# State-space output projection in two passes by token halves, with three transformed inputs made in its second pass

## The chip, the cores and the metric

The kernel runs on one core of a Trainium2 chip. The core has a matrix engine (TensorE, PE in the profile; its weight loads are listed apart as PEld), VectorE (DVE), ScalarE (ACT), GpSimd (POOL) and SyncE (SP), whose queue issues all the DMA transfers. The metric is the time of one execution on the device in microseconds (us).

## The reference

Two transformer-like blocks follow each other on 1024 tokens of width 1024, in 32-bit floats. The part that matters here is in the second block: a state-space branch and an attention branch are projected, gated and merged.

```python
proj = jnp.einsum("bsd,de->bse", h, w_in)
z_ssm, xbc, dt_raw, q, k, v, z_att, f_logit, g_logit = jnp.split(proj, offsets, axis=-1)
y_ssm = _ssd_branch(z_ssm, xbc, dt_raw, conv_w, conv_b, dt_bias, a_log, d_skip, ssm_norm_w)
y_att = _fox_branch(q, k, v, z_att, f_logit, b_f)
g_ssm, g_att = jnp.split(jax.nn.sigmoid(g_logit + b_gate), N_BRANCHES, axis=-1)
merged = g_ssm * jnp.einsum("bse,ed->bsd", y_ssm, w_proj_ssm) + g_att * jnp.einsum("bse,ed->bsd", y_att, w_proj_att)
x = x + gate[:, None, :] * jnp.einsum("bsd,de->bse", merged, w_out)
```

`_ssd_branch` ends with `_rmsnorm(y * silu(z), ssm_norm_w)`. The `gate` above is the last third of `silu(c) @ w_ada + b_ada` (the modulation).

## The kernel before

Activations lie with the 128 channels of a block on the partitions and the 1024 tokens along the free dimension. A product of 32-bit accuracy is made from three fast ones: each operand is split into a high part (rounded, on ScalarE) and a low part (the rest, on VectorE or GpSimd), and `mm3` (three calls of `mm`, L344) adds high*high, high*low and low*high.

**Weights** come as one long list of blocks (`weight_plan`), each [128, 8, 128] (512 KB) for an input width of 1024. `w_load(i)` brings block i into one of two raw buffers once the low part of block i-2 is made. `w_hi(i)` (L328) waits for the load and for the last matmul of block i-2, as there are two buffers for the high parts as well. `w_lo(i)` (L335, here on GpSimd) waits for `w_hi(i)`. `lin(i, hf, ...)` gives the 24 matmuls of block i for one half of the tokens (512).

**The order** within each engine is written out by hand; engines meet at semaphores. A function like `w_hi(PSM[n] + 2)` in a list makes its engine wait there, and whatever stands behind it waits as well. PSUM has eight banks, handed out in turn (`next_bank`); a bank is free once the engine that reads it has read it.

**The state-space output projection** (`stage_ssm_out`) follows the scan (`stage_ssd`). TensorE multiplies the gate block `GS` for both halves, each followed by one matmul that sums squares for the norm (`total`), and then the eight blocks of the projection, `PSM[0]` to `PSM[7]`, each for both halves. ScalarE first makes the high parts of the 16 scaled inputs (L2536), then for each half the sigmoid of the gate (L2543) and the norm factor `rstd` (Ln at L409, Exp at L411), with a split of weights between the halves, and then one `w_hi` per block. VectorE makes the 16 low parts (L2558), scales each product out of PSUM (L2570) and adds up the modulation in eight steps (`ada_step`, L428 and L431), whose sums TensorE makes with eight small matmuls after block 5 (`ada_sums`, read at L446). Results go to DRAM (`md`), one store per half block.

**The gathering stage** (`stage_seven`) computes nine pairs of blocks of `w_in` (attention gate z, and gate logits). Each pair is a product of [2 halves of width] x [2 blocks] by [2 halves of width] x [2 halves of tokens], made with seven products instead of eight: P1, P2, P7, P6, P4, P3, P5. A product is 12 matmuls of 512 tokens. P1, P2 and P3 use the input as it is; P7, P6, P4 and P5 use transformed inputs, sums and differences of its quadrants (`quadrant` L2700, `combine` L2706 on VectorE, `x_hi` L2711 on ScalarE, `x_lo` L2717 on VectorE), which are made once and serve all nine pairs. The weights are summed likewise (`weight_add`, VectorE) and split (`weight_hi` L2685 on ScalarE, `weight_lo` L2691 on GpSimd) into four slots. P7's transformed input is made in the projection stage after block 5; P6, P4 and P5 are made in the gathering stage, as their buffers lie where the projection's split inputs `YS` lie. To bridge that, the order of products starts with P1, P2, P7 of pair 0 and then of pair 1. The load of pair 1 (`pair_load(1)`, L2646) waits for the end of the projection.

Of the kernel before, what the change touches and what calls it, by code (L numbers as in the profile page):

```python
# [43 lines left out]
def weight_plan():  # L44
# [65 lines left out]
    add("gs", W, None, 1024, (G_LOG, G_LOG + 128))  # L110
    full("ps", "w_proj_ssm_2", None, 1024, 0, 8)
# [79 lines left out]
def program(nc, io, table):  # L191
    xT, pT, wflat, wada, vecs, rows, cst, abias, tabs, out = io
    stack = ExitStack()
    with stack:
# [2316 lines left out]
        YS = Y([P, 8, T], F32R), Y([P, 8, T], F32R)  # L2511

        def stage_ssm_out():
            GS, PSM = BLK["gs"][0], BLK["ps"]
            T_ = tmps([((n, hf), (f"md{(2 * n + hf) % 4}", n, hf)) for n in range(8) for hf in range(2)])
# [16 lines left out]

            def scalar():
                for hf in range(2):
                    for k in range(8):
                        ac.activation(YS[0][:, k, half(hf)], XS[:, k, half(hf)], ACT.Identity, scale=v("ssn", k)).then_inc(*on.up(ac, "uh", "S", k, hf))  # L2536
                for hf in range(2):
                    if hf:
                        w_hi(GS + 2)
                    to, before = T_[0, hf]  # L2540
                    on.wait_ge(ac, "mm", GS, hf)
                    on.wait_ge(ac, *before)
                    ac.activation(to, ps[:, bank[GS, hf], :], ACT.Sigmoid, bias=bgn[:, 0:1]).then_inc(*on.up(ac, "gate s", hf))  # L2543
                    rstd("S", hf, bank["S", hf], RA, T)
                for n in range(8):
                    w_hi(PSM[n] + 2)
                    if n == 6:
                        for j in range(2):
                            x_hi("P7", j)
                        for x in range(2):  # L2550
                            weight_hi(x)
                on.ends(ac, "end ssm", "ac")

            def vector():
                for hf in range(2):
                    for k in range(8):
                        on.wait_ge(dv, "uh", "S", k, hf)
                        dv.scalar_tensor_tensor(YS[1][:, k, half(hf)], XS[:, k, half(hf)], v("ssn", k), YS[0][:, k, half(hf)], ALU.mult, ALU.subtract) \  # L2558
                            .then_inc(*on.up(dv, "ul", "S", k, hf))
                for n in range(8):  # L2560
                    for hf in range(2):
# [919 lines left out]
```

## Time and profile before

| What | Value |
|---|---|
| Median of 3 runs | 2794.96 us (2793.74 to 2798.78) |
| The profiled execution, its own time | 2794.93 us |
| Its span, first to last instruction | 2793.6 us |
| TensorE (PE) busy | 2697.8 us, 97% |
| VectorE (DVE) busy | 1683.9 us, 60% |
| ScalarE (ACT) busy | 1388.7 us, 50% |
| GpSimd (POOL) busy | 910.7 us, 33% |
| TensorE's mean granted clock | 0.990 |

The granted clock is TensorE's clock as a share of 2.4 GHz; it has two levels, 1.2 and 2.4 GHz. Matmuls are pipelined and their ends are modelled, so busy times of PE overlap; its gaps are what to look at. Times in the rows are counted from the first instruction.

### The profile page before, as it was taken

Reading aid. Unit: us, or ns where it says so; the run is one execution under the profiler, and the core shown is the slowest. Engines: PE = TensorE matmul, PEld = TensorE weight load, DVE = VectorE, ACT = ScalarE, POOL = GpSimd, SP = SyncE. Lnnn points to the kernel's source line nnn. Section 1 sums busy time; section 2 is a strip of 40 time slices with the busy share of each in tenths; the row PEclk is TensorE's granted clock in tenths of the full one; section 3 lists DMA queues with packets and bytes.
Section 4 is the critical chain, followed back from the end, with each engine's and each line's share of the span. In section 5 each row is a group of like instructions: output and inputs, shape, how many; then the busy total and the mean of one; then the engine's idle time right before and its main releaser. Section 6 shows DMA issues by size and latency. Waiting matters only on the chain.

```text
span 2793.6 us, 36562 instructions
## 1 busy us (share of the span) xinstructions
PE 2697.8 (97%) x13692; PEld 2250.3 (81%) x13692; DVE 1683.9 (60%) x2861; ACT 1388.7 (50%) x2550; POOL 910.7 (33%) x745
## 2 busy tenths in 40 slices
PE   8999989999999999999998999998999999999997
PEld 7878878777788888888886778777788888888886
DVE  6767775643288888887557875556552444443344
ACT  5768864435367767775346335542442343334222
POOL 0434441223366655563122221123541111111431
PEclk9999999999999999999999999999999999999999
DMA  3101132221100000003211310033342110010242
GB/s 136 42 31 42 42 125 70 85 83 39 38 13 10 11 11 10 11 31 113 74 48 35 114 38 23 23 128 106 113 147 93 47 33 29 31 31 31 83 151 76
DMA packets 62367, 167.68 MB, mean 60 GB/s; under 512 B 7024, under 2 KB 15856, under 8 KB 61040
## 3 DMA queue, kind: packets, MB, share of 16 engines
q1 hardware_dynamic: 62192, 165.34, 17.3%
q8 instruction: 111, 1.82, 0.3%
q14 instruction: 64, 0.52, 0.1%
HBM read 139.10 MB, written 26.21 MB: 59 GB/s over the span
## 4 chain that ended last, share of the span: by engine, by line
PE 88%; DVE 5%; ACT 3%; POOL 2%; issue 1%; DMA 0%; POOLq 0%; ACTq 0%; DVEq 0%
PE ps L344 82%; PE ps L462 4%; PE ps L3012 1%; PE ps L788 1%; ACT t L328 1%; POOL t L1328 1%; POOL t L1332 1%; POOL t L1780 0%; DVE t L3370 0%; DMA t<-in_wflat 0%; DVE t L2338 0%; DVE t L919 0%; DVE t L888 0%; POOL t L1330 0%; DVE t L1907 0%
## 5 line engine op out<-in xcount | busy, mean ns | idle before, releaser
L344 PE MATMUL ps<-t,t 128*128 128x512 f32 (+8 forms) x11804 | 2539.4, 374 | 71.3 <-POOL t L2691 10.3
L344 PEld LDWEIGHTS ps<-t,t 128*128 128x128 f32 (+4 forms) x11804 | 2049.5, 185 | 491.4 <-issue 67.4
L335 POOL TENSOR_TENSOR t<-t,t 128x1024 fp32r<-128x1024 f32 (+2 forms) x151 | 323.8, 2145 | 1102.8 <-ACT t L328 746.8
L328 ACT ACTIVATE t<-t 128x1024 fp32r<-128x1024 f32 (+2 forms) x187 | 167.9, 898 | 413.0 <-PE ps L344 412.5
L1720 DVE TENSOR_TENSOR t<-ps,t 128x512 fp32r<-128x512 f32 x256 | 164.6, 684 | 33.2 <-ACT t L1628 32.0
L1780 POOL TENSOR_SCALAR t<-t,t 128x1024 f32<-128x1024 f32 x128 | 144.3, 1127 | 118.7 <-DVE t L1726 113.7
L462 PE MATMUL ps<-t,t 128*128 128x128 f32 x1176 | 157.5, 274 | 11.9 <-POOL t L1780 9.6
L462 PEld LDWEIGHTS ps<-t,t 128*128 128x128 f32 x1176 | 132.4, 140 | 31.1 <-issue 15.2
L1733 DVE TENSOR_REDUCE t<-ps 128x1 f32<-128x1024 f32 x128 | 154.2, 1205 | 0.6 <-PE ps L344 0.6
L1636 ACT ACTIVATE t<-ps,t 128x1024 f32<-128x1024 f32 x128 | 143.0, 1117 | 3.5 <-DVE t L1733 3.3
L1628 ACT ACTIVATE t<-ps 128x512 fp32r<-128x512 f32 x256 | 139.1, 591 | 9.8 <-PE ps L462 5.8
L2691 POOL TENSOR_TENSOR t<-t,t 128x512 fp32r<-128x512 f32 x63 | 90.1, 1437 | 88.8 <-ACT t L2685 88.8
L966 POOL TENSOR_SCALAR t<-t,t 128x384 f32<-128x384 f32 (+1 forms) x128 | 69.6, 564 | 126.5 <-DVE t L913 126.5
L1267 POOL TENSOR_TENSOR t<-t,t 128x512 f32<-128x512 f32 x31 | 49.7, 1604 | 143.2 <-DVE t L1176 143.2
L3135 DVE TENSOR_TENSOR t<-ps,t 128x128 fp32r<-128x128 f32 (+3 forms) x64 | 48.4, 757 | 73.9 <-ACT t L3048 73.8
L2685 ACT ACTIVATE t<-t 128x512 fp32r<-128x512 f32 x63 | 39.0, 629 | 79.6 <-PE ps L344 47.4
L827 ACT ACTIVATE t<-t,t 128x384 f32<-128x384 f32 (+1 forms) x128 | 73.9, 581 | 3.3 <-DVE t L897 2.8
L1328 POOL TENSOR_TENSOR t<-t,t 32x512 f32<-32x512 f32 x34 | 43.7, 1287 | 75.7 <-DVE t L1323 75.5
L3048 ACT ACTIVATE t<-ps 128x128 fp32r<-128x128 f32 (+3 forms) x64 | 41.8, 653 | 51.6 <-PE ps L3012 51.6
L2474 ACT ACTIVATE t<-ps,t 128x128 f32<-128x128 f32 x128 | 34.9, 384 | 59.0 <-PE ps L344 52.9
L888 DVE CUSTOM_DVE_ANT_0 t<-ps,t 128x384 f32<-128x384 f32 (+1 forms) x128 | 61.2, 519 | 4.1 <-PE ps L344 3.4
L335 DVE TENSOR_TENSOR t<-t,t 128x1024 fp32r<-128x1024 f32 (+1 forms) x36 | 31.6, 879 | 46.8 <-ACT t L328 46.7
(245 smaller groups left out, 2538.8 us busy)
## 6 DMA issues: line engine op xcount, KB each, us to landing
t<-in_wflat SPq DMA_DIRECT2D x138, 512.0 KB, 3.6
t<-in_wada SPq DMA_DIRECT2D x48, 256.0 KB, 4.8
t<-in_wflat SPq DMA_DIRECT2D x9, 1024.0 KB, 5.9
t<-in_xT SPq DMA_DIRECT2D x16, 512.0 KB, 7.3
md<-t SPq DMA_DIRECT2D x30, 256.0 KB, 2.7
t<-md SPq DMA_DIRECT2D x30, 256.0 KB, 3.9
t<-in_wflat SPq DMA_DIRECT2D x32, 128.0 KB, 2.0
hd<-t SPq DMA_DIRECT2D x8, 512.0 KB, 3.1
```

The costliest lines, as they stand in the source:

```text
L328: ac.activation(parts(i)[0][:, 0:n], raw[i % 2][:, 0:n], ACT.Copy).then_inc(*on.up(ac, "whi", i))
L335: e.tensor_tensor(lo[:, 0:n], raw[i % 2][:, 0:n], hi[:, 0:n], ALU.subtract) \
L344: return pe.matmul(o, l, r, start=start, stop=stop)
L462: t = pe.transpose(o[:, c * P:(c + 1) * P], src[:, c * P:(c + 1) * P], ident)
L827: ac.activation(S[:, r, 0:nk], S[:, r, 0:nk], ACT.Exp, bias=M[:, 8 + r:9 + r], accum_out=M[:, 16 + r:17 + r]) \
L1328: po.tensor_tensor(ta[64:96], ta[64:96], tb[64:96], ALU.add).then_inc(*on.up(po, "roped", *key, 0))
L1628: ac.activation(to, src, ACT.Copy).then_inc(*on.up(ac, "b pT_hi", i - 3, c))
L1636: ac.activation(Pm[u][:, :], o, ACT.Exp, bias=bm[:, c0:c0 + 1], accum_out=bm[:, c0 + 1:c0 + 2]).then_inc(*on.up(ac, "b exp", i - 1))
L1720: dv.tensor_tensor(to, src, turned(i - 3, c, 0)[0], ALU.subtract).then_inc(*on.up(dv, "b pT_lo", i - 3, c))
L1733: dv.tensor_reduce(bm[:, c0:c0 + 1], o, AX, ALU.max, negate=True).then_inc(*on.up(dv, "b max", i))
L1780: po.tensor_scalar(Pm[u][:, :], Pm[u][:, :], bm[:, c0 + 2:c0 + 3], 1.0, ALU.mult, ALU.mult).then_inc(*on.up(po, "b probs", i - 1))
L2691: po.tensor_tensor(lo[:, :, :], weight(p, W_QUAD[q]), hi[:, :, :], ALU.subtract).then_inc(*on.up(po, "seven_po", p, q))
```

## The change

The projection runs in two passes, one for each half of the tokens. In a pass come the gate block, the sum of squares and the eight projection blocks, each for its half alone (`half_block`, 24 matmuls). The weight list therefore has the gate block and the eight projection blocks twice. The split inputs `YS` become two pairs of buffers, one for each half, so that the first half's buffers are free after the first pass; the transformed inputs P6 and P4 lie there, and are made in the second pass after P7. Only P5 is made in the gathering stage. The order of products becomes the plain one, pair after pair. Both `pair_load(0)` and `pair_load(1)` are issued in the second pass. The slots for split weights move, so that only the first is free before the projection ends: only P1's weights are split ahead.

```diff
-    add("gs", W, None, 1024, (G_LOG, G_LOG + 128))
-    full("ps", "w_proj_ssm_2", None, 1024, 0, 8)
+    for hf in range(2):
+        add("gs", W, None, 1024, (G_LOG, G_LOG + 128))
+        full("ps", "w_proj_ssm_2", None, 1024, 0, 8)
...
-        YS = Y([P, 8, T], F32R), Y([P, 8, T], F32R)
+        YS = [(Y([P, 8, H], F32R), Y([P, 8, H], F32R)) for _ in range(2)]
...
+            def half_block(i, hf, hi, lo, need, frees):
+                nk, m, wh, wl = block(i)
+                b = bank[i] = next_bank(*every)
+                on.wait_ge(pe, "whi", i)
+                on.wait_ge(pe, low(i), i)
+                wait_bank(b)
+                for k in range(8):
+                    for event in need(k, hf):
+                        on.wait_ge(pe, *event)
+                    t = mm3(ps[:, b, :], wh[:, k, :], wl[:, k, :], hi(k), lo(k), k == 0, k == 7)
+                t.then_inc(*on.up(pe, "mm", i, 1))
+                freed[b] = frees
...
             def tensor():
                 for hf in range(2):
-                    bank[GS, hf] = lin(GS, hf, next_bank(*every), Uh, Ul, need_c, [("gate s", hf)])
+                    half_block(GS[hf], hf, lambda k: Uh[:, k, half(hf)], lambda k: Ul[:, k, half(hf)], need_c, [("gate s", hf)])
                     bank["S", hf] = next_bank(*every)
                     total("S", hf, bank["S", hf], RA, ("acc", "S", 7, hf))
-                for n in range(8):
-                    for hf in range(2):
-                        bank[PSM[n], hf] = lin(PSM[n], hf, next_bank(*every), *YS, need_y, [("ssm", n, hf)])
-                    if n == 5:
-                        ada_sums(next_bank(*every))
+                    for n in range(8):
+                        half_block(PSM[n + 8 * hf], hf, lambda k: YS[hf][0][:, k, :], lambda k: YS[hf][1][:, k, :], need_y, [("ssm", n, hf)])
+                        if hf and n == 0:
+                            ada_sums(next_bank(*every))
+                    on.ends(pe, "ssm half", hf)
...
             def scalar():
 ...
                 for hf in range(2):
-                    if hf:
-                        w_hi(GS + 2)
                     to, before = T_[0, hf]
-                    on.wait_ge(ac, "mm", GS, hf)
+                    on.wait_ge(ac, "mm", GS[hf], 1)
                     on.wait_ge(ac, *before)
-                    ac.activation(to, ps[:, bank[GS, hf], :], ACT.Sigmoid, bias=bgn[:, 0:1]).then_inc(*on.up(ac, "gate s", hf))
+                    ac.activation(to, ps[:, bank[GS[hf]], :], ACT.Sigmoid, bias=bgn[:, 0:1]).then_inc(*on.up(ac, "gate s", hf))
                     rstd("S", hf, bank["S", hf], RA, T)
-                for n in range(8):
-                    w_hi(PSM[n] + 2)
-                    if n == 6:
-                        for j in range(2):
-                            x_hi("P7", j)
-                        for x in range(2):
-                            weight_hi(x)
+                    w_hi(GS[hf] + 2)
+                    for n in range(8):
+                        w_hi(PSM[n + 8 * hf] + 2)
+                        if hf and n in (2, 4, 6):
+                            for j in range(2):
+                                x_hi({2: "P7", 4: "P6", 6: "P4"}[n], j)
+                weight_hi(0)
...
             def vector():
...
+                for n, hf in users:
...
+                    dv.tensor_tensor(to, ps[:, bank[PSM[n + 8 * hf]], :], by, ALU.mult).then_inc(*on.up(dv, "ssm", n, hf))
+                    if hf == 0:
+                        ada_step(n)
+                    elif n == 1:
                         ada_out()
                         for j in range(2):
                             quadrant((1, 1), j, "P7", fh)
                             quadrant((0, 1), j, "P7", fl)
                             combine("P7", j, fh["P7"], fl["P7"], ALU.subtract)
+                    elif n == 2:
+                        for j in range(2):
+                            quadrant((0, 0), j, "P6", fh)
+                            combine("P6", j, fl["P7"], fh["P6"], ALU.add)
                         weight_add(0, "P7")
+                    elif n == 3:
                         for j in range(2):
                             x_lo("P7", j)
+                    elif n == 4:
+                        for j in range(2):
+                            quadrant((1, 0), j, "P4", fl)
+                            combine("P4", j, fl["P4"], fl["P6"], ALU.subtract)
+                    elif n in (5, 6):
+                        for j in range(2):
+                            x_lo({5: "P6", 6: "P4"}[n], j)
...
             def gpsimd():
                 for hf in range(2):
-                    if hf:
-                        w_lo(po, GS + 2)
+                    w_lo(po, GS[hf] + 2)
...
+                    for n in range(8):
+                        if hf and n == 7:
+                            weight_lo(0)
+                        w_lo(po, PSM[n + 8 * hf] + 2)
...
             def sync():
+                w_load(GS[0] + 4)
+                on.wait_ge(sp, "ul", "S", 7, 1)
+                for k in range(3):
+                    ada_load(k)
+                for n, hf in users:
+                    if (n, hf) == (0, 1):
+                        w_load(GS[1] + 4)
+                    w_load(PSM[n + 8 * hf] + 4)
+                    on.wait_ge(sp, "ssm", n, hf)
+                    sp.dma_start(md[n, :, half(hf)], T_[n, hf][0]).then_inc(*on.landed(sp, f"md{n % 4}", n, hf))
+                    if hf == 0 and n < 5:
+                        ada_load(n + 3)
+                    if hf and n in (1, 2):
+                        pair_load(n - 1)
...
-        ORDER = [(p, q) for q in ("P1", "P2", "P7") for p in (0,)] + [(1, "P1"), (1, "P2"), (1, "P7")]
-        ORDER += [(p, q) for q in PRODUCTS[3:] for p in range(2)] + [(p, q) for p in range(2, len(SEVEN)) for q in PRODUCTS]
+        ORDER = [(p, q) for p in range(len(SEVEN)) for q in PRODUCTS]
...
             def scalar():
-                for x in range(2, 4):
+                for x in range(1, 4):
                     weight_hi(x)
...
             def vector():
                 for j in range(2):
+                    quadrant((1, 1), j, "P5", fh)
+                    if j == 0:
+                        weight_add(0, "P6")
+                    dv.tensor_tensor(two(fl["P5"], j), two(xl["P6"], j), two(xh["P6"], j), ALU.add) \
                         .then_inc(*on.up(dv, "seven_dv/again", j))
                     on.wait_ge(dv, "seven_dv/again", j)
+                    combine("P5", j, fh["P5"], fl["P5"], ALU.subtract)
                 for x, (p, q) in enumerate(ORDER):
                     if x + 5 < len(ORDER):
                         weight_add(*ORDER[x + 5])
+                    if x == 2:
+                        for j in range(2):
+                            x_lo("P5", j)
                     add(p, q)
```

## Rows read from the trace of the kernel before

**Rows 1.** The page's chain that ended last, by engine, shares of the span.

```profile
PE 88%; DVE 5%; ACT 3%; POOL 2%; issue 1%; DMA 0%; POOLq 0%; ACTq 0%; DVEq 0%
```

**Rows 2.** Timeline of PE, 1812 to 2200: start, length, what, count, [idle before, releaser].

```profile
1823.79 109.76 PE L344 MATMUL ps<-t,t 128*128 128x512 f32 x476 [2.93 <-DVE t L2394]
1934.50 3.02 PE L344 MATMUL ps<-t,t 128*128 128x512 f32 x12 [0.94 <-POOL t L2691]
1942.38 11.35 PE L344 MATMUL ps<-t,t 128*128 128x512 f32 x36 [4.87 <-POOL t L2691]
1957.71 10.06 PE L344 MATMUL ps<-t,t 128*128 128x512 f32 x36 [3.98 <-POOL t L2691]
...
1968.32 180.67 PE L344 MATMUL ps<-t,t 128*128 128x512 f32 x798 [0.54 <-POOL t L2691]
```

**Rows 3.** Timeline of all engines, where VectorE reads modulation sums and the last product.

```profile
1906.23 0.17 DVE L446 TENSOR_TENSOR t<-ps,t 128x8 f32<-128x8 f32 x1 [0.99 <-PE ps L344]
...
1928.15 0.69 DVE L2570 TENSOR_TENSOR t<-ps,t 128x512 f32<-128x512 f32 x1 [2.17 <-PE ps L344]
```

**Rows 4.** Timeline of all engines at the projection stage's start.

```profile
1828.13 9.94 ACT L2536 ACTIVATE t<-t,t 128x512 fp32r<-128x512 f32 x16 [0.81 <-DVE t L2413]
...
1832.67 5.68 PEld L344 LDWEIGHTS ps<-t,t 128*128 128x128 f32 x25 [0.24 <-issue]
1838.08 1.28 ACT L2543 ACT_TABLE_LOAD   x1
...
1839.02 94.11 PEld L344 LDWEIGHTS ps<-t,t 128*128 128x128 f32 x423 [0.24 <-issue]
1839.38 0.69 ACT L2543 ACTIVATE t<-ps,t 128x512 f32<-128x512 f32 x1
...
1843.92 1.05 ACT L328 ACTIVATE t<-t 128x1024 fp32r<-128x1024 f32 x1
...
1845.43 2.40 POOL L335 TENSOR_TENSOR t<-t,t 128x1024 fp32r<-128x1024 f32 x1
```

**Rows 5.** The same timeline, load of pair 1 and its first user.

```profile
1933.59 0.48 SPq L2646 DMA_DIRECT2D t<-in_wflat  x1
...
1940.36 0.63 ACT L2685 ACTIVATE t<-t 128x512 fp32r<-128x512 f32 x1 [10.56 <-DMA t<-in_wflat]
```

**Rows 6.** Windows: length, busy us (count) of PE, PEld, DVE, ACT, POOL, granted clock, DMA share, GB/s.

```profile
1824.00:1826.00 2.00, 2.00 (x5) 1.58 (x6) 2.00 (x5) 0.00 (x0) 0.00 (x0) 0.50 0.00 0
1860.00:1870.00 10.00, 10.00 (x46) 8.29 (x45) 6.86 (x8) 1.06 (x1) 2.40 (x1) 1.00 0.79 254
```

**Rows 7.** Timeline of ACT in the scan stage, a table load and its first use.

```profile
1800.29 1.28 ACT L2474 ACT_TABLE_LOAD   x1
1802.17 2.18 ACT L2474 ACTIVATE t<-ps,t 128x128 f32<-128x128 f32 x8 [0.59 <-PE ps L344]
```

**Rows 8.** Timeline of all engines, end of one projection block and the next split.

```profile
1882.79 0.69 DVE L2570 TENSOR_TENSOR t<-ps,t 128x512 f32<-128x512 f32 x1 [3.43 <-PE ps L344]
1882.85 1.07 ACT L328 ACTIVATE t<-t 128x1024 fp32r<-128x1024 f32 x1 [9.82 <-PE ps L344]
...
1883.99 2.41 POOL L335 TENSOR_TENSOR t<-t,t 128x1024 fp32r<-128x1024 f32 x1 [8.47 <-ACT t L328]
```

**Rows 9.** The same timeline, VectorE and GpSimd together, then each alone (1936.70 and 1941.06).

```profile
1929.36 2.88 POOL L335 TENSOR_TENSOR t<-t,t 128x1024 fp32r<-128x1024 f32 x1 [4.00 <-ACT t L328]
1930.02 3.30 DVE L2847 TENSOR_TENSOR t<-t,t 128x1024 f32<-128x1024 f32 x1
1932.20 2.25 POOL L2691 TENSOR_TENSOR t<-t,t 128x512 fp32r<-128x512 f32 x1
...
1936.70 1.22 DVE L2847 TENSOR_TENSOR t<-t,t 128x1024 f32<-128x1024 f32 x1
...
1941.06 1.27 POOL L2691 TENSOR_TENSOR t<-t,t 128x512 fp32r<-128x512 f32 x1 [6.62 <-ACT t L2685]
```

**Rows 10.** Groups by line and form, 1826 to 1990: count | busy, mean ns | idle before.

```profile
L2700 DVE TENSOR_TENSOR t<-t,t 128x1024 f32<-128x1024 f32 x10 | 15.4, 1538 | 0.1
```

More of the change, by code:

```diff
@@ L2510, in program @@
         Y = region(YO)
-        YS = Y([P, 8, T], F32R), Y([P, 8, T], F32R)
+        YS = [(Y([P, 8, H], F32R), Y([P, 8, H], F32R)) for _ in range(2)]
         def stage_ssm_out():
-            GS, PSM = BLK["gs"][0], BLK["ps"]
-            T_ = tmps([((n, hf), (f"md{(2 * n + hf) % 4}", n, hf)) for n in range(8) for hf in range(2)])
+            GS, PSM = BLK["gs"], BLK["ps"]
+            users = [(n, hf) for hf in range(2) for n in range(8)]
+            T_ = tmps([((n, hf), (f"md{n % 4}", n, hf)) for n, hf in users])
             need_y = lambda k, hf: [("uh", "S", k, hf), ("ul", "S", k, hf)]
@@ L2626, in program @@
         S7 = region(OO + 16384)
-        slots = [(S7([P, 4, P], F32R), S7([P, 4, P], F32R)) for _ in range(2)]
-        pair_raw = [S7([P, 2 * T])]
+        pair_raw = [S7([P, 2 * T]) for _ in range(2)]
         S7 = region(YO + 49152)
-        pair_raw.append(S7([P, 2 * T]))
-        slots += [(S7([P, 4, P], F32R), S7([P, 4, P], F32R)) for _ in range(2)]
         scaled = [S7([P, H]) for _ in range(2)]
+        spare = [(S7([P, 4, P], F32R), S7([P, 4, P], F32R)) for _ in range(4)]
+        slots = [spare[3]] + spare[0:3]
         tiles = [t[:, :] for t in tmp] + [RA[:, half(hf)] for hf in range(2)]
-        ORDER = [(p, q) for q in ("P1", "P2", "P7") for p in (0,)] + [(1, "P1"), (1, "P2"), (1, "P7")]
-        ORDER += [(p, q) for q in PRODUCTS[3:] for p in range(2)] + [(p, q) for p in range(2, len(SEVEN)) for q in PRODUCTS]
+        ORDER = [(p, q) for p in range(len(SEVEN)) for q in PRODUCTS]
         def pair_load(p):
-            if p == 0:
-                on.wait_ge(sp, "ul", "S", 7, 1)
-            elif p == 1:
-                on.wait_ge(sp, "end ssm", "pe")
+            if p < 2:
+                on.wait_ge(sp, "sums/ada", 2)
             else:
@@ L2676, in weight_hi @@
                 on.wait_ge(ac, "mm/seven", *ORDER[x - 4])
-            elif x < 2:
-                on.wait_ge(ac, "sums/ada", 2)
-            else:
+            elif x:
                 on.wait_ge(ac, "end ssm", "pe")
@@ L2696, in quadrant @@
         def quadrant(x, j, q, to):
+            if q in ("P6", "P4"):
+                on.wait_ge(dv, "ssm half", 0)
             kh, hf = x
@@ L2738, in before_tile @@
                     return [stored[y][mine - 1]]
-                return [(f"md{x}", 6 if x < 2 else 7, x % 2) for x in range(4)] + [("ssm", 7, 1)]
+                return [(f"md{x}", 4 + x, 1) for x in range(4)] + [("ssm", 7, 1)]
             def tensor():
@@ L2778, in scalar @@
             def scalar():
-                for x in range(2, 4):
+                for x in range(1, 4):
                     weight_hi(x)
-                for j in range(2):
-                    x_hi("P6", j)
-                    ac.activation(two(kept, j), two(fl["P6"], j), ACT.Copy).then_inc(*on.up(ac, "seven_ac/keep", j))
                 for x, (p, q) in enumerate(ORDER):
@@ L2789, in scalar @@
                     if x == 1:
-                        for j in range(2):
-                            x_hi("P4", j)
-                    if x == 4:
                         for j in range(2):
@@ L2875, in gpsimd @@
             def gpsimd():
-                for x in range(2, len(ORDER)):
+                for x in range(1, len(ORDER)):
                     weight_lo(x)
@@ L2880, in sync @@
             def sync():
-                pair_load(1)
                 for x in range(4):
-                    on.wait_ge(sp, f"md{x}", 6 if x < 2 else 7, x % 2)
+                    on.wait_ge(sp, f"md{x}", 4 + x, 1)
                 for g in range(2):
```

66 lines of the change are left out of this document (14 added, 52 removed).

## The prediction

> **What bounds the kernel now.** I read the chain that ended last first: TensorE is 88% of it, 82% by the one line that issues the three-term matmuls [rows 1]. So the edit pays or costs by what it does to gaps and clock of TensorE, since it removes no matmul. Next TensorE's timeline around the change [rows 2]. From 1823.79 it runs without a gap through the whole projection and into the gathering stage. Then come gaps of 0.94, 4.87, 3.98 and 0.54 us, and after 1968.32 none for 180 us: 798 matmuls in 180.67 us, 0.2264 us each. One half block (24 matmuls) is thus 5.43 us and one product of the gathering stage (12) 2.72 us.
>
> The projection's last product is taken by VectorE at 1928.15 [rows 3], so TensorE left it at 1928.1; what runs on to 1933.5 are P1 and P2 of pair 0, whose weights were split early. From 1928.1 to 1968.3 are 40.2 us for 2 + 12/12 + 36/12 + 36/12 = 9 products, 24.5 us of work. **15.7 us are lost at the start of the gathering stage**: this is what the edit can win back. 10.3 are gaps. The rest is clock: 36 matmuls took 11.35 and 10.06 us after the long gaps [rows 2] for 8.15 at full rate. The 4.87 us gap is the load of pair 1, issued at 1933.59 and used by ScalarE at 1940.36 [rows 5]; the 3.98 us gap stands before the first P6.
>
> **Part A: one half block instead of two before block 1.** In the stage's first 15 us TensorE has the gate block's first half (to 1832.25, a total to 1832.67), its second half and total (to 1839.02) [rows 4]. These, and the first projection block's two halves, now cover ScalarE, which makes 16 scaled inputs (1828.13 to 1838.07), then table load, sigmoid, table load, Ln, table load, Exp, and only then splits the next weights (1843.92) [rows 4]. In the new order TensorE has only one gate half and one projection half ahead of that split. It is done at 1832.67 + 5.43, with a little for the inputs' arrival 1838.4. The new order puts the split behind the whole gate chain, where it already stands for this first one, and GpSimd now takes the low part before the gate's product: high part 1843.92 to 1844.97, low part 2.40 us long [rows 4], ready at 1847.5. **Gap 9.1 us.** Nothing covers it: the block after is behind it in order. Then the clock: it was at its lower level (0.50, 1.2 GHz) when TensorE resumed at 1823.79 [rows 6], after a gap of 2.93 us [rows 2]; the gate half took 8.46 us for 5.43, a loss of 3.0, and after 4.87 and 3.98 us the losses were 3.2 and 1.9 [rows 2]. I take 2.7. Sum of A: 11.8 us.
>
> **Double weight work in pass 1.** Nine more blocks of 512 KB: nine splits of 1.06 us on ScalarE and 2.40 on GpSimd, and nine loads on SP. Before, both came once per 10.9 us; now each 5.43. After the matmul two blocks earlier ends, the high part takes 0.06 + 1.07, the low one follows at 1.20 and ends at 3.61 us [rows 8], against 5.43 needed. Both are hidden, with 1.8 us to spare. A load leaves 3.6 us after one block's end and is used two blocks later, 7.3 us on. Per block now go 512 KB of weights, 512 of modulation and 256 of output; the window from 1860 moved 254 GB/s at a DMA share of 0.79 [rows 6], hence an estimated 321 GB/s when full, 4.1 us for 1.31 MB. So the double loads are costed at nothing; what they cost if that cover goes is rival 3.
>
> **Part B: the second gate.** The gate half ends, and sigmoid to end of low part is 1839.38 to 1844.97 plus 0.1 plus 2.40 = 8.1 us [rows 4]. Its first table load comes before its wait, as at 1800.29, where the load stands ahead of 0.59 us of waiting for TensorE [rows 7]. TensorE has a total (0.42), one half (5.43) and the modulation sums (1.7: read at 1906.23, after 0.99 us of waiting and 0.69 for the product before them [rows 3]) to set against it: 7.55. Gap 0.6 us, and no clock is lost (0.94 and 0.54 cost next to none [rows 2]).
>
> **Part C: VectorE's new work in pass 2.** It makes P7 (six operations), P6 and P4 (four each) and their low parts (six): 20 of 128x1024 at 1.22 us each when alone [rows 9], 24.4 us, beside GpSimd's 2.40 us split now in every block. The rows show how the two meet. GpSimd's split from 1929.36 took 2.88 us, the VectorE operation issued at 1930.02 took 3.30 for 1.22 and ended 1.08 us after the split's end, and GpSimd's 1.27 us operation [rows 9] of 1932.20 took 2.25. They take turns whole. So while both have work VectorE gets one or two operations per block.
> The Trainium skill, SBUF — State Buffer, "SBUF: two separate sides", says that the pair of ports which the two share is an exclusive lock, and that the loser blocks for the full instruction when VectorE's operation has two SBUF inputs. By this rule the sum comes to the 2810.7 below, and without it to the 2799.4 of rival 1; the rows of contention here agree with it.
> By the mean of the grouped row (1.54 us, [rows 10]) P7 would take 9.2 us and VectorE nearly keep up. By turns it takes 12.1. Block 8 ends at 1847.5 + 2.7 + 9 x 5.43 + 0.4 = 1899.5 and block 9, which starts after the gap of part B at 1901.8, at 1907.3. VectorE takes that product and the sums, starts P7 at 1908.2, gives way at 1909.5 and 1914.2 for 2.4 us each, and ends it at 1920.2. ScalarE has P7's high part queued ahead of the split for block 13, and that split wanted to start at 1918.2. Behind P7's second high part it starts at 1921.3, GpSimd waits out one more VectorE operation, and the low part is there at 1925.9. TensorE is done at 1923.6. **Gap 2.3 us**, clock loss between none (0.94 us gap) and 1.9 (3.98 us gap): 0.8. Later splits wait one VectorE operation at most, 3.61 + 1.22 = 4.8 us after the block's end of 5.43, and are hidden. The projection then ends at 1925.9 + 3 x 5.43 = 1942.2, 1943.0 with the clock: 14.9 us later than 1928.1 (A, B and C give 15.5; the rest is rounding of the blocks before).
>
> **Part D: the start of the gathering stage.** Here the 15.7 us go, and other waits come. By the same turns (one or two operations of 1.22 us, then one split of 2.40) VectorE still owes P4, two pairs of low parts and three products when TensorE ends; P4 is done 2.6 us after that end. ScalarE's P4 high part, the split of the next stage's weights (1.06) and P1's high part (0.6), each queued behind the other, end 5.2 us after it. P1's low part on GpSimd, 1.27 and up to 1.22 behind VectorE, makes 7.0: before, P1 and P2 ran at once. Next, P2's weights stand behind a 2.40 us split: 1.0 more beyond a P1 at low clock. P6's weight sum adds 0.2. VectorE's backlog pushes P5's inputs, and behind them the sum for P3's weights, to some 28 us after the end: gap 3.4. P5's low part 0.7. Clock after the 7.0: 2.7; after the 3.4: 1.0. Sum 16.0, against 15.7 now: +0.3. From pair 1 on, whose load is now early (issued in pass 2), all is as before.
>
> **Sum.** A 11.8 + B 0.6 + C 3.1 + D 0.3 = 15.8 us on the profiled execution's 2794.93 (span 2793.6), which is the median of the three runs to 0.03 us: 2810.7.
>
> **The rivals.** Rival 1, VectorE keeps up, by the grouped mean of 1.54 us. Then there is no gap in C, and D is P1's split chain behind block weights (1.06 + 0.1 + 0.6 + 1.27, 3.1 us), 2.7 of clock and some 2 for P2 and P6: 7.8, 7.9 less than now. Result 12.4 - 7.9 = +4.5, 2799.4. For it: that mean is what these operations took here. Against it: GpSimd worked less often when they did. It decides once VectorE ends its list with TensorE: some 10 us less than by turns.
> Rival 2, not slower: the gathering stage's start loses nothing, all seven transformed inputs and weights waiting when TensorE comes. The 15.7 us come back whole, and A and B take 12.4: -3.3, 2791.6, within 0.2%. The start may lose up to 15.7 - 12.4 + 5.6 = 8.9 us before the result is slower by 0.2%. Against it: P2's high part still waits for the stage's end by its own line, and VectorE's list is 25 us long without any turn taken.
> Rival 3, pass 1 starves: weights come late while the modulation loads share the queue. It bites from 7.3 us between issue and landing; each of five blocks then waits about 1 us: 2816, and with VectorE's backlog growing to two operations more, 2819. For it: the share of 0.79 with half the weights. Against: 4.1 us of 5.43.
>
> **Chances.** Forecast 0.61 (own range 2805 to 2817: A's clock by 1, C's 0 to 1.9, D by 4). Rival 1 0.17, rival 2 0.09, rival 3 0.13. Range 2797 to 2820, which leaves out rival 2 and the ends of the rest. A change of 0.2% is 5.6 us, about what a measurement can tell from none. Slower holds the forecast, rival 3 and half of rival 1: 0.83. The same holds the rest of rival 1 and most of rival 2: 0.13. Faster 0.04.
>
> **What would show it.** In the changed kernel's trace: a TensorE gap of about 9 us ended by GpSimd's low part near 1847.5, with low clock after it; one under 1 us near 1902; one of 2 to 3 us near 1924, with ScalarE waiting for VectorE's P7; then about 7 us at the first product of the gathering stage and 3 us at its sixth; no wait for a pair's load. If instead the first gap is under 6 us, ScalarE's order is not what I read. If VectorE's transforms average 1.3 us, rival 1 holds. A load that TensorE waits for in pass 1 is rival 3.

## The result, and the profile after

The changed kernel took 2805.49 us (median of 6 runs, 2803.69 to 2806.65) against 2796.03 us for the kernel before (6 runs, 2793.74 to 2798.78): a ratio of 1.0033, 95% interval 1.002 to 1.0046, 9.5 us more. The forecast was 2811, 15.8 more, with 2797 to 2820 as its range: slower as said, by three fifths of the amount.

TensorE's timeline after the change, to be read against [rows 2] (start, length, what, count, [idle before, releaser]):

```profile
1825.88 14.40 PE L345 MATMUL ps<-t,t 128*128 128x512 f32 x50 [2.92 <-DVE t L2395]
1849.68 76.36 PE L345 MATMUL ps<-t,t 128*128 128x512 f32 x330 [9.40 <-POOL t L336]
1927.30 16.56 PE L345 MATMUL ps<-t,t 128*128 128x512 f32 x72 [1.26 <-ACT t L329]
1948.21 16.70 PE L345 MATMUL ps<-t,t 128*128 128x512 f32 x60 [4.35 <-POOL t L2708]
1967.55 193.08 PE L345 MATMUL ps<-t,t 128*128 128x512 f32 x846 [2.65 <-POOL t L2708]
```

Look for four gaps. Two stand in the projection, where there was none before: TensorE waits 9.40 us for GpSimd's low part of block 1, and 1.26 us at block 13. Two stand at the start of the gathering stage, where there were four before: 4.35 us for P1's low part and 2.65 us for P3's. (Blocks are counted as in the prediction: 0 to 7 are the first pass's eight projection blocks, 8 to 15 the second pass's.) Both kernels do the same products from the gate block's first matmul to the gathering stage's last one, so this stretch can be laid side by side: 1968.32 + 180.67 - 1823.79 = 325.20 us before [rows 2], 1967.55 + 193.08 - 1825.88 = 334.75 us after, 9.55 more. This is the measured difference of the medians. The profiled spans differ by 11.7 us (2793.6 and 2805.3), 2.1 more, since the stretch began at 1825.88 instead of 1823.79: nothing is changed ahead of it, and the start varied between 1822.89 and 1827.70 over the profiles below. So I compare stretches, and medians beside them.

The place of the first gap, all engines, to be read against [rows 4]:

```profile
1830.21 9.93 ACT L2552 ACTIVATE t<-t,t 128x512 fp32r<-128x512 f32 x16 [0.81 <-DVE t L2414]
...
1840.16 1.28 ACT L2557 ACT_TABLE_LOAD   x1
1841.45 0.69 ACT L2557 ACTIVATE t<-ps,t 128x512 f32<-128x512 f32 x1
...
1845.99 1.99 ACT L329 ACTIVATE t<-t 128x1024 fp32r<-128x1024 f32 x2
1847.19 2.34 POOL L336 TENSOR_TENSOR t<-t,t 128x1024 fp32r<-128x1024 f32 x1 [24.53 <-ACT t L329]
```

ScalarE has work without a pause from 1830.21 to 1847.98, and block 1's split stands at the end of its list. TensorE had done block 0 at 1840.28 and waits for the low part at 1849.53. And the second pass, where VectorE and GpSimd meet:

```profile
1910.44 4.55 DVE L2719 TENSOR_TENSOR t<-t,t 128x1024 f32<-128x1024 f32 x2
1910.96 2.95 POOL L336 TENSOR_TENSOR t<-t,t 128x1024 fp32r<-128x1024 f32 x1 [3.44 <-ACT t L329]
...
1916.16 4.55 DVE L2719 TENSOR_TENSOR t<-t,t 128x1024 f32<-128x1024 f32 x2
...
1916.40 3.23 POOL L336 TENSOR_TENSOR t<-t,t 128x1024 fp32r<-128x1024 f32 x1 [2.49 <-ACT t L329]
...
1920.75 1.23 DVE L2725 TENSOR_TENSOR t<-t,t 128x1024 f32<-128x1024 f32 x1
...
1922.01 1.06 ACT L2730 ACTIVATE t<-t 128x1024 fp32r<-128x1024 f32 x1 [4.67 <-DVE t L2725]
...
1922.97 1.04 ACT L329 ACTIVATE t<-t 128x1024 fp32r<-128x1024 f32 x1
...
1946.10 1.65 ACT L2702 ACTIVATE t<-t 128x512 fp32r<-128x512 f32 x3
1946.79 1.36 POOL L2708 TENSOR_TENSOR t<-t,t 128x512 fp32r<-128x512 f32 x1 [3.72 <-ACT t L2702]
```

Two VectorE operations of 1.22 us each take 4.55 where a split by GpSimd falls among them, and GpSimd's split of 2.40 takes 2.95 and 3.23. ScalarE waits 4.67 us for P7 (1922.01) with block 13's split behind it (1922.97). The same meeting is seen in VectorE's making of P4, twice in this stretch:

```profile
1935.62 2.82 DVE L2719 TENSOR_TENSOR t<-t,t 128x1024 f32<-128x1024 f32 x1
...
1940.86 3.30 DVE L2725 TENSOR_TENSOR t<-t,t 128x1024 f32<-128x1024 f32 x1
```

Grouped over 1826 to 1990, the quadrants took 2.17 us each where [rows 10] had 1.54:

```profile
L2719 DVE TENSOR_TENSOR t<-t,t 128x1024 f32<-128x1024 f32 x10 | 21.7, 2168 | 0.1
```

### The profile page after: what moved, and what is told of

It reads as the page before. It is cut to its first block, busy times and chain, and to the rows that moved or that the text cites. A ratio compares the mean times of both kernels' runs of the same rounds, so it can differ in the third digit from the quotient of the medians.

```text
span 2805.3 us, 36614 instructions
## 1 busy us (share of the span) xinstructions
PE 2704.1 (96%) x13692; PEld 2253.8 (80%) x13692; DVE 1693.5 (60%) x2861; ACT 1396.1 (50%) x2557; POOL 933.9 (33%) x754
## 3 DMA queue, kind: packets, MB, share of 16 engines
q8 instruction: 111, 1.82, 0.3%
## 4 chain that ended last, share of the span: by engine, by line
PE 84%; DVE 6%; POOL 4%; ACT 3%; issue 2%; DMA 1%; SPq 0%; POOLq 0%; DVEq 0%; ACTq 0%
PE ps L345 77%; PE ps L463 4%; PE ps L3018 1%; POOL t L336 1%; PE ps L789 1%; DMA t<-md 1%; DVE t L2719 1%; ACT t L329 1%; DMA t<-gd 1%; POOL t L1329 1%; POOL t L1333 1%; POOL t L1781 0%; DVE t L3376 0%; ACT t L2552 0%; DVE t L2725 0%
## 5 line engine op out<-in xcount | busy, mean ns | idle before, releaser
L336 POOL TENSOR_TENSOR t<-t,t 128x1024 fp32r<-128x1024 f32 (+2 forms) x160 | 350.0, 2188 | 1121.9 <-ACT t L329 764.9
L329 ACT ACTIVATE t<-t 128x1024 fp32r<-128x1024 f32 (+2 forms) x196 | 177.1, 905 | 401.3 <-PE ps L345 400.8
```

The costliest lines, as they stand in the source:

```text
L329: ac.activation(parts(i)[0][:, 0:n], raw[i % 2][:, 0:n], ACT.Copy).then_inc(*on.up(ac, "whi", i))
L336: e.tensor_tensor(lo[:, 0:n], raw[i % 2][:, 0:n], hi[:, 0:n], ALU.subtract) \
```

## The experiments

All stand beside runs of the kernel before on the same chip, so two kernels are compared by their ratios, or by each one's distance from the kernel before, and not by their bare medians. "Stretch" is the 325.20 us above, of the one profiled run. Edits are shown against the changed kernel.

| Kernel | Median, us | Before beside it | Ratio (95%) | Stretch, against before |
|---|---|---|---|---|
| changed kernel | 2805.49 | 2796.03 | 1.0033 (1.002 to 1.0046) | +9.55 |
| e1_split_first | 2794.97 | 2796.44 | 0.9997 (0.9988 to 1.0006) | -1.10 |
| e2_fill_gap | 2812.16 | 2796.44 | 1.0058 (1.0045 to 1.0072) | +10.60 |
| e2b_fill_same_bank | 2805.91 | 2795.59 | 1.0033 (1.0021 to 1.0045) | +8.96 |
| e3_short_lows | 2799.34 | 2796.44 | 1.0013 (1.0004 to 1.0022) | +3.23 |
| e4_passes_alone | 2809.37 | 2796.44 | 1.005 (1.0038 to 1.0063) | +13.61 |
| e5_start_order | 2809.82 | 2795.59 | 1.0051 (1.0038 to 1.0063) | +12.18 |
| e5b_load_out_of_way | 2803.78 | 2794.63 | 1.0033 (1.0021 to 1.0046) | +7.63 |
| e7_all_orders | 2800.81 | 2795.59 | 1.0016 (1.0008 to 1.0025) | +1.82 |
| e7b_all_orders_2 | 2791.22 | 2794.63 | 0.9987 (0.9978 to 0.9996) | -5.75 |
| e8_p7_high_later | 2804.99 | 2795.59 | 1.0032 (1.002 to 1.0045) | +9.53 |

**Is the first gap ScalarE's order?** The splits of blocks 1 and 2 go ahead of the gate chain, in the second pass that of block 9 does too, and GpSimd's low parts follow in the same order.

```diff
                 for hf in range(2):
                     for k in range(8):
...
+                    w_hi((GS[0], PSM[0])[hf] + 2)
                 for hf in range(2):
+                    if hf:
+                        w_hi(GS[1] + 2)
...
                     rstd("S", hf, bank["S", hf], RA, T)
-                    w_hi(GS[hf] + 2)
```

> The changed kernel with ScalarE's order alone altered: the splits of weight blocks 1 and 2 stand behind the first and the second eight scaled inputs, ahead of the gate chain; in pass 2 block 9's split stands ahead of the gate chain too (GpSimd's low parts follow in the same order). Theory 1 (the 9.4 us gap is ScalarE's order and nothing else): 8 inputs end 5.0 us after 1830.2, high part 1.06, low part 2.4, so block 1 is ready near 1838.8 + 0.1, before TensorE ends block 0 at 1840.3: gap 0, and with no gap no low clock, so 9.4 + 2.6 = 12.0 us less than the changed kernel, some 2.5 us less than the kernel before; the rest (1.3 us at block 13, start of the gathering stage 11.6 us lost) as it was. Rival (the weights' load or SP's queue stands right behind the split): the gap shrinks only to 4 to 6 us, for the load of block 3 is then what is late. Rival 2 (clock falls whatever the gap): only 9.4 us less.

```profile
1826.16 25.18 PE L345 MATMUL ps<-t,t 128*128 128x512 f32 x98 [2.93 <-DVE t L2395]
1852.14 5.72 PE L345 MATMUL ps<-t,t 128*128 128x512 f32 x24 [0.80 <-issue]
1859.09 57.44 PE L345 MATMUL ps<-t,t 128*128 128x512 f32 x258 [1.23 <-issue]
```

```profile
1855.47 1.06 ACT L329 ACTIVATE t<-t 128x1024 fp32r<-128x1024 f32 x1 [6.25 <-DMA t<-in_wflat]
```

In e1's timeline of TensorE the 9.40 us and the low clock after it are gone; 0.80 and 1.23 us have come in their place, of which the second is the load of block 4 (ScalarE waited 6.25 us for it, to 1855.47), issued behind six modulation loads. The stretch is 10.65 us shorter than the changed kernel's: 12.0 were expected, and 2.0 went to the new gaps. The expectation's first rival, a late load right behind the split, was right about the mechanism and not about its size or its block. The order on ScalarE, and on GpSimd behind it, was worth the whole of the change's net loss: with it mended the kernel is as fast as before.

**Is the gap's second cost the clock?** 38 matmuls that nobody reads fill it.

```diff
+                        if hf == 0 and n == 0:
+                            b = next_bank(*every)
+                            wait_bank(b)
+                            for x in range(38):
+                                mm(ps[:, b, :], idr[:, :], YS[0][0][:, 0, :], x == 0, x == 37)
+                            freed[b] = []
```

> The changed kernel with 38 more matmuls (identity by one scaled input, into a bank nobody reads) after block 0 of pass 1, inside the 9.4 us gap; they add nothing to the output. Theory 1 (the gap's second cost is TensorE's clock, low since it stood still): the clock stays at its upper level, blocks 1 to 3 take 5.43 us each, block 1 ends 8.4 us after block 0's end of waiting instead of 10.7, 2.6 us less than the changed kernel. Rival (block 1's 8.1 us come from waiting for its second operand or from load traffic, not the clock): nothing changes, or it is slower by what the fill overlaps the weights' arrival.

This did not answer the question: `next_bank` moved the turn of the banks for every stage that follows, there was a wait of 1.47 us late in the gathering stage that no other profile has, and the kernel came out 15.7 us slower than before. With the bank kept (`b = every[(turn[every] + 1) % 8]`, and no change to `freed`):

> As e2_fill_gap, but the 38 filling matmuls go into the bank that block 1 then takes and overwrites, so that the turn of the banks in all later stages is that of the changed kernel. Theory 1 (clock): the gap is filled, block 1 takes 5.4 to 5.7 us instead of 8.1, and the stretch from the gate block's start to the attention stage is 1.5 to 2.6 us shorter than the changed kernel's 336.75; e2's later losses (a wait of 1.47 us in the gathering stage and 2.5 us after it) are gone, for they came with the shifted banks. Rival (the fill itself costs later, by load on the memory or the clock): the later losses stay.

Windows (length, busy us and count of PE, PEld, DVE, ACT, POOL, granted clock, DMA share, GB/s), first of the changed kernel, then of e2b:

```profile
1850.00:1854.00 4.00, 4.00 (x10) 3.11 (x10) 0.74 (x2) 0.00 (x0) 3.10 (x2) 0.50 0.77 257
```

```profile
1849.00:1853.00 4.00, 4.00 (x19) 3.31 (x18) 1.10 (x2) 0.00 (x0) 2.86 (x2) 1.00 0.89 285
...
1901.00:1904.00 3.00, 3.00 (x10) 2.33 (x9) 0.69 (x1) 0.00 (x0) 2.83 (x2) 0.57 0.61 175
```

At a clock of 0.50 TensorE began 10 matmuls in 4 us, at 1.00 it began 19. So the clock was the gap's second cost, 8.1 us for block 1 against 5.43. But the stretch is only 0.6 us shorter, not 1.5 to 2.6: the clock now fell at 1901, where in the changed kernel it had stayed up (below), and the medians show no gain at all. The wait of e2 is gone, as expected. Of e2's loss behind the gathering stage 1.5 us are gone, and 1.0 is left against the changed kernel (643.7 us from the attention stage's start to the end, for 645.2 in e2 and 642.7 in the changed kernel; the last section shows where clock was lost there).

**Do VectorE and GpSimd take turns?** The low parts of blocks 10 to 15 are made for 16 columns only; the rest of them is left out.

```diff
                 hi, lo = parts(i)
+                if i in BLK["ps"][10:16]:
+                    n = 16
```

> The changed kernel with the low parts of the weights of blocks 10 to 15 (pass 2) made for 16 of 1024 columns alone; the rest of these low parts is left out, so GpSimd's 2.4 us splits vanish from the stretch in which VectorE makes P7, P6 and P4. Theory 1 (VectorE and GpSimd take turns, whole instructions long): P7's six operations take 7.4 us instead of 11.5, the 1.26 us gap at block 13 is gone, VectorE's list ends before TensorE does, and the start of the gathering stage loses 3.1 us of gap and 2.6 of clock, 5.7 instead of 11.6: 7 us less in all. Rival (VectorE's list is long by itself, no turns): P7 stays near 11 us, at most 1 us less in all.

```profile
1908.44 2.48 DVE L2721 TENSOR_TENSOR t<-t,t 128x1024 f32<-128x1024 f32 x2
...
1910.95 1.23 DVE L2727 TENSOR_TENSOR t<-t,t 128x1024 f32<-128x1024 f32 x1
1912.09 2.48 DVE L2721 TENSOR_TENSOR t<-t,t 128x1024 f32<-128x1024 f32 x2
...
1914.61 1.23 DVE L2727 TENSOR_TENSOR t<-t,t 128x1024 f32<-128x1024 f32 x1
...
1943.70 15.50 PE L347 MATMUL ps<-t,t 128*128 128x512 f32 x60 [3.33 <-POOL t L2710]
```

P7 takes 7.4 us, 1908.44 to 1915.84, for 11.5; block 13 waits no more; the gathering stage's first gap is 3.33 us (3.1 expected) for 4.35. The stretch is 6.3 us shorter than the changed kernel's (7 expected). So GpSimd's splits are what makes VectorE's list long, and the two take turns, as the prediction said; what one turn costs VectorE was 2.1 us and not 2.4.

**What do the passes cost alone, and what do the early transforms repay?**

The projection keeps its two passes; the order of products, the buffers, the load of pair 1 and the making of P6 and P4 go back to those of the kernel before.

```diff
-                        if hf and n in (2, 4, 6):
+                        if hf and n == 6:
                             for j in range(2):
-                                x_hi({2: "P7", 4: "P6", 6: "P4"}[n], j)
-                weight_hi(0)
+                                x_hi("P7", j)
+                            for x in range(2):
+                                weight_hi(x)
...
-        ORDER = [(p, q) for p in range(len(SEVEN)) for q in PRODUCTS]
+        ORDER = [(p, q) for q in ("P1", "P2", "P7") for p in (0,)] + [(1, "P1"), (1, "P2"), (1, "P7")]
+        ORDER += [(p, q) for q in PRODUCTS[3:] for p in range(2)] + [(p, q) for p in range(2, len(SEVEN)) for q in PRODUCTS]
```

> The two passes alone: the kernel before, with its order of products, its buffers, and P6, P4 and P5 made in the gathering stage, but the projection in two passes with the weights loaded twice, P7 made after block 9. Theory 1 (the passes cost, the early transforms repay): TensorE's gap of 9.4 us before block 1 and 2.6 us of clock stay, no gap at block 13, and the start of the gathering stage loses what it lost before, 15.7 us: 12 us more than the kernel before, 2.5 us more than the changed kernel. Rival (early transforms do not repay, their gain is lost at VectorE): 9.5 us more than the kernel before or less, that is no slower than the changed kernel.

```profile
1849.41 92.81 PE L345 MATMUL ps<-t,t 128*128 128x512 f32 x402 [9.27 <-POOL t L336]
1942.69 5.74 PE L345 MATMUL ps<-t,t 128*128 128x512 f32 x24 [0.48 <-POOL t L2705]
1950.56 3.01 PE L345 MATMUL ps<-t,t 128*128 128x512 f32 x12 [2.13 <-POOL t L2705]
1957.77 11.35 PE L345 MATMUL ps<-t,t 128*128 128x512 f32 x36 [4.19 <-POOL t L2705]
1973.10 10.06 PE L345 MATMUL ps<-t,t 128*128 128x512 f32 x36 [3.98 <-POOL t L2705]
```

Against the kernel before it takes 13.6 us more in the stretch, 12.9 in the median: 9.27 us before block 1 and its clock, then gaps of 0.48, 2.13, 4.19, 3.98 and 0.55 us at the start of the gathering stage, 11.3 where the kernel before had 10.3. The early transforms, with the order of products and the loads that go with them, repay 4.1 us in the stretch, 3.5 in the medians (12.9 and 9.5). So they bring more than their gap at block 13 costs; the loss is that of the passes.

**Are the waits at the gathering stage's start queue order?** P1's weights go ahead of P4's high part, the next stage's split behind P6's, P3's sum between P5's halves.

```diff
+                        if hf and n == 6:
+                            weight_hi(0)
...
                 for x in range(1, 4):
                     weight_hi(x)
+                w_hi(PSM_LAST + 2)
...
-                    if j == 0:
-                        weight_add(0, "P6")
+                    weight_add(0, ("P6", "P3")[j])
```

> The changed kernel with the orders at the start of the gathering stage alone altered: P1's weights are split ahead of P4's high part (after block 14), the split of the next stage's weight block comes after the splits of P2, P7 and P6, and the sum for P3's weights is made between the two halves of P5. Theory 1 (the 4.35 us at P1 and the 2.65 us at P3 are queue order on ScalarE, GpSimd and VectorE): no wait at P1 and no low clock there, 0.5 us at P2, about 1 at P6, 2.5 to 3.5 at P5, which still comes late; some 5.5 us lost in place of 11.6, so 6 us less than the changed kernel. Rival (VectorE's backlog of 8.6 us past the end of the projection is what counts): the wait moves from P1 to P7 or P6 whole, and less than 2 us are won.

```profile
1943.66 8.45 PE L345 MATMUL ps<-t,t 128*128 128x512 f32 x36 [1.48 <-POOL t L2711]
1955.06 4.60 PE L345 MATMUL ps<-t,t 128*128 128x512 f32 x12 [2.95 <-POOL t L2711]
1965.94 195.71 PE L345 MATMUL ps<-t,t 128*128 128x512 f32 x858 [6.28 <-POOL t L2711]
```

The expectation was wrong: 2.6 us more in the stretch than the changed kernel instead of 6 less. The gap at P1 fell to 1.48, and 6.28 us came at P4. All engines there:

```profile
1958.34 0.33 SPq L318 DMA_DIRECT2D t<-in_wflat  x1
1958.71 0.43 SPq L2635 DMA_DIRECT2D md<-t  x1
...
1963.42 0.60 ACT L2790 ACTIVATE t<-ps 128x512 f32<-128x512 f32 x1 [9.07 <-DMA md<-t]
```

ScalarE's copy of P1's product waits 9.07 us for the last store to `md`. That store was ready since 1950.9 and stood in SP's queue behind a weight load, which waited for the very split that I had moved to later. The P4 and P3 splits stood behind the copy. With the load moved behind it:

```diff
                 for g in range(2):
                     md_load(g)
+                w_load(PSM_LAST + 4)
```

> As e5_start_order, with one difference: the load of weight block FV0, which in SP's queue stood ahead of the last store to md, comes after the two md loads of the gathering stage. Theory 1 (e5's 6.28 us at P4 is ScalarE's copy of P1's product waiting for that store, which SP held behind a load waiting for the split of FK0 that e5 had moved to later): the copy no longer waits for a DMA, the gap at P4 falls below 1.5 us and the low clock behind it goes; some 6 to 8 us less than e5 (2809.8), 2802 to 2804. Rival (P5's transform on VectorE sets the pace whatever else): the wait moves to P3 or P5 and less than 3 us are won.

```profile
1955.37 4.59 PE L345 MATMUL ps<-t,t 128*128 128x512 f32 x12 [2.95 <-POOL t L2712]
1960.88 5.82 PE L345 MATMUL ps<-t,t 128*128 128x512 f32 x24 [0.92 <-POOL t L2712]
1968.26 188.87 PE L345 MATMUL ps<-t,t 128*128 128x512 f32 x834 [1.55 <-POOL t L2712]
```

The gap at P4 is 0.92 us and the low clock behind it is gone, which settles the cause of e5's loss. The stretch is 4.55 us shorter than e5's. Each set against the kernel before beside it, the medians differ by 5.1 us (9.15 and 14.23 more than it), a little under the 6 to 8 expected. Against the changed kernel the orders win 1.9 us in the stretch, not 6, and only 0.3 in the medians: 2.95 us at P6 remain, whose sum stands behind VectorE's backlog, and 1.55 at P5. The gaps at the gathering stage's start add up to 6.87 us for the changed kernel's 7.00; they have moved, and what was won is clock. So e5's rival, the backlog, holds for the larger part, and the queue's order for the rest.

**Is block 13's gap the split queued behind P7?** P7's high part goes one block later.

```diff
-                        if hf and n in (2, 4, 6):
+                        if hf and n in (3, 4, 6):
```

> The changed kernel with P7's high part on ScalarE moved one block later, behind the split of block 13. Theory 1 (the 1.26 us gap at block 13 is that split queued behind P7): the gap is gone, VectorE's list is as long as before, so 1.3 us less at that place and about as much less in all. Rival (GpSimd's low part is late anyway, behind VectorE's turns): a gap of 0.5 us or more stays.

```profile
1849.09 92.65 PE L345 MATMUL ps<-t,t 128*128 128x512 f32 x402 [9.46 <-POOL t L336]
1947.63 16.73 PE L345 MATMUL ps<-t,t 128*128 128x512 f32 x60 [5.89 <-POOL t L2708]
```

The gap is gone, and nothing is won: 402 matmuls in one piece, and then 5.89 us before P1 instead of 4.35. TensorE finished the projection 1.5 us earlier, counted from its start, and met the same VectorE. The stretch is that of the changed kernel to 0.02 us. A wait that is hidden behind a later one has no price.

**All orders together.** e1, e8 and e5 at once, block 3's split between Ln and Exp, and block 4's load ahead of the modulation.

```diff
+                    if hf == 0:
+                        w_hi(PSM[1] + 2)
                     on.wait_ge(ac, "ln", "S", hf)
...
                 w_load(GS[0] + 4)
+                w_load(PSM[0] + 4)
```

> All orders together: as e1_split_first, with block 3's split between Ln and Exp and the load of block 4 ahead of the modulation loads (e1 had gaps of 0.80 and 1.23 us there), as e8_p7_high_later, and as e5_start_order. Theory 1: no gap in the projection, 2.0 us less than e1 there and 1.3 at block 13, and 5 to 6 less at the start of the gathering stage: 8 us less than e1, 2787 to 2789, 8 to 9 less than the kernel before. Rival (the parts are not additive, since a faster TensorE leaves VectorE's list further behind at the end): only e1's result less 3 to 4 us.

It held e5's fault, 6.26 us at P4, and came out 5.2 us above the kernel before instead of 8 to 9 below. Mended like e5b, with the splits of P2 and P7 ahead of P4's high part, two modulation blocks loaded at first instead of three, and the sums for P6 and P3 made in the projection stage (P6's ahead of P4's low parts; P3's came behind them, though the expectation says ahead):

```diff
+                        if hf and n == 7:
+                            weight_hi(1)
+                            weight_hi(2)
...
+                        if n == 6:
+                            weight_add(0, "P6")
...
-                for k in range(3):
+                for k in range(2):
                     ada_load(k)
```

> As e7_all_orders, with that load moved behind the twelfth product, the split of FK0 moved behind the tenth, the splits of P2's and P7's weights ahead of P4's high part, the sums for P6's and P3's weights ahead of VectorE's last low parts, and two modulation blocks loaded at first instead of three. Theory 1: no gap from the projection's start to P4, one at P5, whose transform VectorE ends about 20 us after the projection's end against 16.3 of products before it: 3 to 7 us and up to 3 of clock. That is 2789 to 2792, 4 to 7 less than the kernel before and 9 to 12 less than e7. Rival (VectorE's backlog only moves on): the gap at P5 is over 9 us, and the result within 2 us of the kernel before.

```profile
1822.89 36.12 PE L345 MATMUL ps<-t,t 128*128 128x512 f32 x146 [2.93 <-DVE t L2395]
1859.28 68.32 PE L345 MATMUL ps<-t,t 128*128 128x512 f32 x306 [0.27 <-issue]
1928.23 8.46 PE L345 MATMUL ps<-t,t 128*128 128x512 f32 x36 [0.63 <-POOL t L2733]
1938.38 3.01 PE L345 MATMUL ps<-t,t 128*128 128x512 f32 x12 [1.70 <-POOL t L2733]
1945.44 196.90 PE L345 MATMUL ps<-t,t 128*128 128x512 f32 x858 [4.05 <-POOL t L2733]
```

It takes 0.9987 of the kernel before (0.9978 to 0.9996), 3.4 us less in the median; the 5.75 us less in the stretch are those of a profiled run near the low end of its eleven (2789.23 us, median 2791.22). So the two passes are a little better than the kernel before once the orders fit them. Whether orders of this kind would speed up the kernel before as well was not run. I had expected one gap, at P5; instead 1.70 us stand at P6 and 4.05 at P4, where ScalarE's copy of P1's product waited 5.49 us for the last store to `md`, whose product VectorE scales behind all of P4's low parts.

## Why the prediction was right, and where it was off

The measured 2805.49 lies in the stated range, just inside the forecast's own 2805 to 2817, and about as far from the forecast's 2810.7 as from rival 1's 2799.4. The number alone does not tell the two apart. The trace and e3 do: VectorE's quadrant operations averaged 2.17 us and not 1.54 in the changed kernel, and P7 took 7.4 us for 11.5 once GpSimd's splits were out of the way. Part by part:

- **Part A**, 11.8 us: 9.40 of gap (9.1 said) and 2.7 of clock (2.7 said; block 1 ran from 1849.68 to 1857.8, 8.1 for 5.43). e1 shows the cause, e2b the clock.
- **Double weight work in pass 1**, nothing: right. From block 1 to block 12 TensorE runs without a gap of 0.3 us, in 76.36 us: 13 x 5.43 = 70.6 of blocks, 0.4 of a total, 1.6 of modulation sums, 2.7 of clock and 1.1 of small delays; the DMA share reached 0.97 in a window from 1854, and no block waited. Rival 3 did not come, though in e1 and e7, where TensorE reaches these blocks sooner, 1.23 and 1.02 us of waiting for a load did.
- **Part B**, 0.6 us: from the gate half's end (1895.84) to block 9's start (1903.99) are 8.15 us, the split chain's 8.1, against 7.55 of work; as a gap only 0.19 of it shows, the rest lies between the small matmuls.
- **Part C**, 3.1 us: 1.26, and no clock (72 matmuls in 16.56 us for 16.30). The mechanism was as said, P7 at 1921.98 with block 13's split behind it, and e8 shows it by taking the gap away; the size was off, in part because a turn costs VectorE 2.1 us and not 2.4, so that P7 took 11.5 us and not 12.1. The prediction's own [rows 9] had this: 3.30 us for an operation of 1.22 is 2.08 more, not 2.40.
- **Part D is the term that was most off**: "Sum 16.0, against 15.7 now: +0.3". TensorE left the projection at 1943.86. From there to 1967.55 are 23.7 us for five products, 13.6 of work: 10.1 lost, and 1.5 more of clock in the stretch after it (846 matmuls in 193.08 us for 191.5). That is 11.6 instead of 16.0, and against 15.7 before it is 4.1 won. The largest piece is P1's wait, 4.35 us for 7.0, and it goes back to VectorE's backlog: the prediction has P4 done 2.6 us after TensorE's end, and it was done 0.3 us after (1944.16). Six splits by GpSimd fall into VectorE's list up to there. At the prediction's 2.4 us each they would cost it 14.4; in the trace five cost 2.1 to 2.2 us and one 1.6 (2.82 for 1.22), 12.1 in all. That is the size of the difference, though the prediction does not give its count, so the working of the 2.6 cannot be redone to the tenth. The rest: P2's extra 1.0 is hidden in a P1 at low clock (together they lose 2.8 us where 3.7 were given), P5's 0.7 did not come, and P3 waited 2.65 for 3.4.

So: 12.1 + 0.2 to 0.6 + 1.5 - 4.1 = 9.7 to 10.1 us by these terms, 9.55 in the stretch, 9.5 between the medians. Parts C and D were both priced too high, in part by the same turn of 2.4 us, and A 0.3 too low, so the errors hardly cancelled. Rival 1 fell (the quadrants averaged 2.17 us, not 1.54), rival 2 too.

## What to carry to other kernels

When a weight-stationary stage is split into passes, count what stood behind the second half of its first block: here ScalarE's 16 inputs and a chain of three table loads had lain under four half blocks of TensorE and were left with two. Where two engines take turns at whole instructions, price the list of the one by how many of the other's instructions fall into it, each at some 0.3 us less than its own length in these traces, and not by a mean from another stretch. Before a split or a wait is moved, follow what each queue holds behind it: e5 lost 4.6 us of its stretch because SP's next load waited for the moved split and a store waited behind the load.

## What the runs showed of the hardware

The granted clock fell where TensorE had hardly stood still. In e2b it was at 0.57 in the window 1901 to 1904 (at the lower level for 3.4 us from 1901.3), after eight one-column matmuls and under 0.2 us without a weight load. In e2 it fell at about the same place of its work (0.59 in the window 1904 to 1908). In the changed kernel the window from 1902 to 1906 shows 1.00, and none of the kernels without the 38 extra matmuls lost clock at these eight. What the extra matmuls have to do with it, some 50 us later, is not shown.

The clock also differed where the work was the same. In every profile a gap of 1.98 or 1.99 us stands before the attention stage's first 80 matmuls; they took 17.80 to 17.82 us in eight profiles, and 19.38 to 19.43 in e2b, e5, e7 and e7b. First the changed kernel, then e2b:

```profile
2162.63 17.80 PE L345 MATMUL ps<-t,t 128*128 128x512 f32 x80 [1.99 <-ACT t L3121]
```

```profile
2160.68 19.38 PE L345 MATMUL ps<-t,t 128*128 128x512 f32 x80 [1.98 <-ACT t L3126]
```

In e5 the window 2164 to 2168 shows a clock of 0.62, in the changed kernel 2163 to 2167 shows 1.00. So a microsecond won by keeping TensorE busy, 2.6 at one place, can be gone at the next: in e2b all but 0.6 of it within the stretch (3.4 us at half the clock are 1.7), and 1.6 more behind it. A difference of 1 to 2 us between two kernels may be no more than this.

A shift of the turn of PSUM banks by one, which changes no amount of work, went with a wait of 1.47 us in the gathering stage and a longer time behind it: e2 takes 645.2 us from the attention stage's start to the end. The other profiles take 642.6 to 644.2; the four longest of them, 643.5 and more, are those with 1.6 us of clock lost there, which e2 has not. What waits on what there was not followed.
